# Cross attention with its exact fp32 products replaced by products of rounded high and low parts

## The chip, the core and the metric
One core of a Trainium2 chip runs the whole program. The metric is the device time of one execution in microseconds; the kernel before takes 1740.92 us (median of 3 runs, 1740.75 to 1741.70). The engines are TensorE (PE, matrix products, with its weight loads PEld), ScalarE (ACT), VectorE (DVE), GpSimd (POOL) and SyncE (SP, which issues the DMAs). They run side by side, each through its own list of instructions in order, and wait for each other with semaphores.

## The reference, cut to what matters
Two transformer blocks on 512 tokens of width 1024, all in fp32. The first has a gated feed-forward, a token mixer, cross attention to a memory of 256 rows, and a second feed-forward, each followed by a layer norm; the second has self attention with pooling and a feed-forward. The change is in the cross attention:

```
def _memory_cross_attention(h, mem, mem_g, mem_b, wq, wk, wv, wo):
    m = _layer_norm(mem, mem_g, mem_b)
    q = (h @ wq).reshape(B, T, 4, 256)
    k = (m @ wk).reshape(B, M, 4, 256)
    v = (m @ wv).reshape(B, M, 4, 256)
    s = jnp.einsum('bthd,bmhd->bhtm', q, k) * (256 ** -0.5)
    p = jax.nn.softmax(s, axis=-1)
    o = jnp.einsum('bhtm,bmhd->bthd', p, v).reshape(B, T, 1024)
    return o @ wo
```

## The kernel before
Activations lie turned: 128 features on the partitions, 512 tokens along the row, eight such tiles to a width of 1024. Every dense layer is a row of *blocks*. A block is one 128-column slice of a weight matrix; its output is one PSUM bank. Operands are kept in two rounded parts (type fp32r), high and low: `ahi` and `alo` for activations, `whi` and `wlo` for weights. A block's product is three rounded products for each of its 8 contraction tiles, 24 in all: `ahi` x `whi`, `alo` x `whi` (L434, L435) and `ahi` x `wlo` (L438); the first two blocks of a layer go together (L461, L462, L467).

Weights stream in by DMA into six slots `wraw`. ACT rounds a block to `whi` (L394, `hi_stream`), three blocks ahead of its use; then POOL (even blocks of these layers) or DVE (odd blocks) subtracts to get `wlo` (L399, `lo_stream`). Block outputs go round through banks 0 to 3; whoever empties a bank counts `bank_free`, and PE waits for it before it reuses the bank.

The stages around the change, in order, are the keys (`mk`, 8 blocks of 256 columns, the memory's rows), the values (`mv`, the same), the queries (`xq`, 8 blocks of 512 columns), the attention head, and the output projection (`xo`). The order of work on each engine is written out by hand.

- *Keys.* After each block DVE copies the bank to `kx` (L1828), makes its `wlo` (odd blocks), and does a piece of the second norm (`second_norm`). That norm is shared: DVE forms the variance (L1409, L1410), ACT takes logarithm and exponential (L1009, L1010); then for each of the 8 feature tiles DVE subtracts the mean (L1413) and multiplies (L1415), ACT applies gain and bias twice (L1015 to `ahi`, L1016 to `res`, "the pair"), and DVE forms `alo` (L1404). The tiles come in rounds 3, 5, 7, 9, 11, 12, 13 and 15 of the sixteen key and value blocks, on ACT one round later.
- *Values.* DVE copies the bank to `vxt` (L1835), PE turns it into bank 4 or 5 (L2298, `turn_values`, one block later), DVE copies the turned block to `vx` (L1839, L1842), counted by `s_kv`.
- *Queries.* DVE copies each block to `qx` with the scale 1/16 (L1874). After block 4 PE makes the scores of head 0, after block 7 it turns the probabilities of head 0.
- *The head.* For each of the four heads, numbered 0 to 3: *scores* (L2311, 8 exact fp32 products of 256 columns, `qx` by `kx`), maxima on DVE (L1847), exponentials on ACT (L1135), normalising on DVE (L1861, L1862), *turning* on PE (L2324, 8 transposes into banks 4 and 5), the turned halves copied to `pxT` (bank 4 by DVE, L1869; bank 5 by ACT, L1149), *attending* on PE (L2336, 4 exact products of 512 columns, `vx` by `pxT`), and its result rounded to `ahi` by ACT (L1143) and `alo` by DVE (L1854). In the trace each exact fp32 product shows as two passes, with two weight loads and two matmul records.

PE's order in the head is: turning 0, scores 1, scores 2, attend 0, turning 1, scores 3, turning 2, attend 1, turning 3, attend 2, attend 3, then xo. ACT's is: half 0, exponentials 1 and 2, attended 0, halves 1 and 2, exponentials 3, attended 1, half 3, attended 2 and 3. DVE's is: half 0, maxima 1, normalise 1, maxima 2, normalise 2, low part of attended 0, half 1, maxima 3, half 2, normalise 3, low part 1, half 3, low parts 2 and 3.

Of the kernel before, what the change touches and what calls it, by code (L numbers as in the profile page):

```python
# [92 lines left out]
def build(nc, A, out):  # L93
    ctx = ExitStack()
    with ctx:
# [110 lines left out]
        take = region(WORK)  # L206
        sst = take("sst", [P, QH, T], F32R)
# [418 lines left out]
        s_pca = sem("probabilities_copied_act")  # L626
        s_pv = sem("attended")
        s_ah = sem("attended_hi")

        s_rope = sem("rope_loaded")  # L630
        s_hsq = sem("head_squares")
# [215 lines left out]
        def _(act):  # L847
# [155 lines left out]
            def second_norm(m):  # L1003

                if m == 2:
                    act.wait_ge(stat_mean, 1)
                    act.activation(var[:, 0, :], mean_of("ln2"), ACT.Square).then_inc(mean_sq, 1)
                    act.wait_ge(var_ready, 1)
                    link(act.activation(rstd[:, :], var[:, 1, :], ACT.Ln, bias=small[:, S_EPS5:S_EPS5 + 1]))  # L1009
                    act.activation(square_mean_of("ln2"), rstd[:, :], ACT.Exp, scale=-0.5).then_inc(rstd_ready, 1)  # L1010
                if m - 1 in LN2_AT:
                    k = LN2_AT[m - 1]
                    act.wait_ge(scaled, k + 1)
                    g, b = vcol(V_LN2G + k), vcol(V_LN2B + k)
                    act.activation(ahi[:, k, :], res[:, k, :], ACT.Identity, bias=b, scale=g).then_inc(hi_act, 1)  # L1015
                    act.activation(res[:, k, :], res[:, k, :], ACT.Identity, bias=b, scale=g).then_inc(normed, 1)  # L1016
# [97 lines left out]
            for j in range(KD):  # L1114
                hi_stream(phases["out"], j)
                square_res(j, phases["out"])
                if j == MEM_AT:

                    act.wait_ge(s_mv, 1)
                    link(act.activation(mrs[:, :], mmv[:, :, 1], ACT.Ln, bias=small[:, S_EPS5:S_EPS5 + 1]))  # L1120
                    act.activation(mrs[:, :], mrs[:, :], ACT.Exp, scale=-0.5).then_inc(s_mr, 1)
                if j == MEM_AT + 1:

                    for k in range(KD):
                        act.wait_ge(s_ma, k + 1)
                        act.copy(mhi[:, k, :], mval[:, k % MVAL, :]).then_inc(s_mh, 1)
            for m in range(2 * KD):
                hi_stream(phases["mk"], m)
                second_norm(m)
            def cross_exp(h):  # L1130
                for t in range(TT):
                    act.wait_ge(s_nm, 2 * h + 2)
                    if t == 0 and h >= 2:
                        act.wait_ge(s_pT, 2 * (h - 1))
                    i = act.activation(px[:, h % 2, t, :], bank[SCORE_BANK[h] + t // 2][:, (t % 2) * MEM:(t % 2 + 1) * MEM],  # L1135
                                       ACT.Exp, bias=small[:, S_NM + 4 * (h % 2) + t:S_NM + 4 * (h % 2) + t + 1],
                                       accum_out=small[:, S_SM + 4 * (h % 2) + t:S_SM + 4 * (h % 2) + t + 1])
                    i.then_inc(s_pe, 1)
# [4 lines left out]
                    act.copy(ahi[:, 2 * h + d, :], bank[ATTEND_BANK[h] + d][:, :]).then_inc(s_ah, 1)  # L1143

            def take_turned(h):
                act.wait_ge(s_pT, 2 * h + 2)
                if h >= 2:
                    act.wait_ge(s_pv, 2 * (h - 1))
                act.copy(pxT[:, h % 2, 1, :], bank[5][:, :]).then_inc(s_pca, 1)  # L1149

            for j in range(KD):
                hi_stream(phases["xq"], j)
                second_norm(2 * KD + j)
                if j == 5:
                    cross_exp(0)
            take_turned(0)
            cross_exp(1)
            cross_exp(2)
# [199 lines left out]
        def _(dve):  # L1358
# [465 lines left out]
                                          vcol(V_MEMG + k), vcol(V_MEMB + k), ALU.mult, ALU.add).then_inc(s_ma, 1)  # L1824

            for j in range(KD):
                wait_block(dve, phases["mk"], j)
                dve.tensor_copy(kx[:, j, :], bank_of(phases["mk"], j)[:, 0:MEM]).then_inc(bank_free, 1)  # L1828
                lo_stream(phases["mk"], j)
                second_norm(j)  # L1830
            for j in range(KD):
                wait_block(dve, phases["mv"], j)
                if j >= 2:
                    dve.wait_ge(s_vxT, j - 1)
                dve.tensor_copy(vxt[:, j % 2, :], bank_of(phases["mv"], j)[:, 0:MEM]).then_inc(bank_free, 1)  # L1835
                lo_stream(phases["mv"], j)
                if j >= 1:
                    dve.wait_ge(s_vxT, j)
                    dve.tensor_copy(vx[:, :, (j - 1) * P:j * P], bank[4 + (j - 1) % 2][:, 0:MEM].rearrange("p (n f) -> p n f", f=P)).then_inc(s_kv, 1)  # L1839
                second_norm(KD + j)  # L1840
            dve.wait_ge(s_vxT, KD)
            dve.tensor_copy(vx[:, :, (KD - 1) * P:KD * P], bank[4 + (KD - 1) % 2][:, 0:MEM].rearrange("p (n f) -> p n f", f=P)).then_inc(s_kv, 1)  # L1842
            def cross_max(h):
                n0 = S_NM + 4 * (h % 2)
                dve.wait_ge(s_sc, h + 1)
# [17 lines left out]
                                      ALU.mult).then_inc(s_pn, 1)  # L1863

            def take_turned(h):
                dve.wait_ge(s_pT, 2 * h + 1)
                if h >= 2:
                    dve.wait_ge(s_pv, 2 * (h - 1))
                dve.tensor_copy(pxT[:, h % 2, 0, :], bank[4][:, :]).then_inc(s_pcd, 1)  # L1869

            for j in range(KD):
                wait_block(dve, phases["xq"], j)
# [130 lines left out]
        def _(pe):  # L2003
# [298 lines left out]
            def cross_scores(h):  # L2302
                if h == 0:
                    pe.wait_ge(bank_free, freed(phases["xq"], 1))
                elif h < 3:
                    pe.wait_ge(bank_free, freed(phases["xq"], last_block_in(phases["xq"], SCORE_BANK[h] + 1)))
                if h >= 2:
                    pe.wait_ge(s_pe, TT * (h - 1))
                for t in range(TT):
                    for k in range(2):  # L2310
                        i = pe.matmul(bank[SCORE_BANK[h] + t // 2][:, (t % 2) * MEM:(t % 2 + 1) * MEM],  # L2311
                                      qx[:, 2 * h + k, t * P:(t + 1) * P], kx[:, 2 * h + k, :], start=(k == 0), stop=(k == 1))
                i.then_inc(s_sc, 1)

            def cross_turn(h):
                pe.wait_ge(s_pn, TT * (h + 1))
                if h:
                    pe.wait_ge(s_pcd, h)
                    pe.wait_ge(s_pca, h)
                else:  # L2320
                    pe.wait_ge(s_kv, KD)
                for m in range(MT):
                    for t in range(TT):
                        i = pe.transpose(bank[4 + m][:, t * P:(t + 1) * P], px[:, h % 2, t, m * P:(m + 1) * P], ident)  # L2324
                    i.then_inc(s_pT, 1)

            def cross_attend(h):
                pe.wait_ge(s_pcd, h + 1)
                pe.wait_ge(s_pca, h + 1)
# [4 lines left out]
                for d in range(2):  # L2334
                    for m in range(MT):
                        i = pe.matmul(bank[ATTEND_BANK[h] + d][:, :], vx[:, m, (2 * h + d) * P:(2 * h + d + 1) * P], pxT[:, h % 2, m, :],  # L2336
                                      start=(m == 0), stop=(m == MT - 1))
                    i.then_inc(s_pv, 1)

            def first_head(j):  # L2340
# [63 lines left out]
            def self_turn(h, st):  # L2404
# [4 lines left out]
                        pe.wait_ge(bank_free, freed(phases["in2"], last_block_in(phases["in2"], 3)))  # L2409

                if st == 2:
                    pe.wait_ge(s_pcd, XH + h + 1)
                elif st == 3:
                    pe.wait_ge(s_pca, XH + 3 * h + 1)
                elif h:
                    pe.wait_ge(s_pca, XH + 3 * (h - 1) + 2 + st)
# [4 lines left out]
            def self_attend(h, st):  # L2421
# [1 line left out]
                if h < 0:  # L2423
                    return
                if st == 0:
                    pe.wait_ge(s_pcd, XH + h + 1)
                    pe.wait_ge(s_pca, XH + 3 * (h + 1))
# [47 lines left out]
```

## Time and profile before
| | |
|---|---|
| median of the runs | 1740.92 us (1740.75 to 1741.70) |
| the profiled execution | 1740.76 us |
| its span, first to last instruction | 1738.90 us, so 1.86 us lie around it |
| busy: PE, PEld, DVE, ACT, POOL | 98%, 82%, 39%, 34%, 41% of the span |
| mean granted clock of TensorE | 0.996 |

A busy share is a mean over stages with different limits. An engine's idle time in front of an instruction is put down to what released it. The chain of waits is followed back from the last instruction, at each step to what released it. In the timeline, rows of equal instructions are merged (x8), the first number is the start and the second the time until the end of the last. Since the matmuls overlap, their pace is read from one start to the next.

### The profile page before, as it was taken

The numbers are of one execution on the slowest core, as the hardware profiler recorded it, in microseconds if no ns is written. First come the engines' busy times: TensorE is split into PE (matmuls) and PEld (weight loads), VectorE is DVE, ScalarE is ACT, GpSimd is POOL, SyncE is SP. The second block draws the span as 40 slices with busy tenths as digits, with TensorE's granted clock in tenths as the row PEclk, the third lists the DMA queues.
The fourth block names the chain that finished last, engine by engine and source line by source line (L and its number), as shares of the span: only waits on it lengthen the run. The fifth ranks groups of instructions, "written<-read, shape, count | busy, mean of one in ns | idle before, by whom it ended". The sixth has DMA issues, their size and how long they took to land.

```text
span 1738.9 us, 21093 instructions
## 1 busy us (share of the span) xinstructions
PE 1701.5 (98%) x8525; PEld 1417.6 (82%) x8525; DVE 681.1 (39%) x1122; ACT 589.5 (34%) x890; POOL 710.9 (41%) x386
## 2 busy tenths in 40 slices
PE   7999999998999999999999999999899999999998
PEld 6888888897888789879888888898657988888886
DVE  3111211268776776356211121266884522112122
ACT  4222222256444554236222222246453422222210
POOL 3443444445554343114453444433331454444442
PEclk9999999999999999999999999999999999999999
DMA  6333243333222345212433233342111333323322
GB/s 189 97 97 97 79 116 97 97 110 85 61 61 61 97 125 142 73 49 71 112 97 97 82 112 97 86 128 61 37 37 49 85 98 97 97 82 112 97 85 73
DMA packets 302826, 157.66 MB, mean 91 GB/s; under 512 B 5145, under 2 KB 301194, under 8 KB 302730
## 3 DMA queue, kind: packets, MB, share of 16 engines
q1 hardware_dynamic: 302730, 156.32, 31.6%
q8 instruction: 68, 1.11, 0.3%
q14 instruction: 28, 0.23, 0.1%
HBM read 154.20 MB, written 2.10 MB: 90 GB/s over the span
## 4 chain that ended last, share of the span: by engine, by line
PE 66%; DVE 4%; ACT 3%; issue 2%; POOL 0%; DVEq 0%; ACTq 0%; POOLq 0%
PE bank L434 16%; PE bank L435 16%; PE bank L438 15%; PE bank L2430 1%; PE bank L2054 1%; PE bank L2051 1%; PE bank L2050 1%; PE bank L481 1%; PE bank L482 1%; PE bank L486 1%; PE bank L2206 1%; PE bank L467 1%; PE bank L461 1%; PE bank L462 1%; PE bank L2311 1%
## 5 line engine op out<-in xcount | busy, mean ns | idle before, releaser
L399 POOL TENSOR_TENSOR wlo<-wraw,whi 128x1024 fp32r<-128x1024 f32 (+1 forms) x256 | 608.6, 2390 | 909.9 <-ACT whi L394 909.9
L434 PE MATMUL bank<-ahi,whi 128*128 128x512 f32 x1312 | 516.0, 393 | 0.0
L435 PE MATMUL bank<-alo,whi 128*128 128x512 f32 x1312 | 511.7, 390 | 0.0
L394 ACT CAST whi<-wraw 128x1024 fp32r<-128x1024 f32 (+1 forms) x286 | 285.9, 1025 | 255.4 <-PE bank L438 169.4
L438 PE MATMUL bank<-ahi,wlo 128*128 128x512 f32 x1312 | 324.0, 389 | 0.0
L434 PEld LDWEIGHTS bank<-ahi,whi 128*128 128x128 f32 x1312 | 247.2, 188 | 52.1 <-issue 1.2
L435 PEld LDWEIGHTS bank<-alo,whi 128*128 128x128 f32 x1312 | 247.0, 188 | 52.0 <-issue 1.2
L438 PEld LDWEIGHTS bank<-ahi,wlo 128*128 128x128 f32 x1312 | 246.3, 188 | 51.1
L1377 DVE SCALAR_TENSOR_TENSOR hval<-gate,bank 128x512 f32<-128x512 f32 x66 | 45.4, 688 | 557.2 <-PE bank L438 543.2
L859 ACT ACTIVATE gate<-bank 128x512 f32<-128x512 f32 x66 | 39.6, 600 | 514.9 <-PE bank L438 506.1
L1386 DVE SCALAR_TENSOR_TENSOR res<-res,bank 128x512 f32<-128x512 f32 x80 | 54.1, 686 | 261.7 <-PE bank L438 181.7
L434 PE MATMUL bank<-hid,whi 128*128 128x512 f32 x332 | 130.5, 393 | 0.0
L435 PE MATMUL bank<-hid,whi 128*128 128x512 f32 x332 | 129.9, 391 | 0.0
L438 PE MATMUL bank<-hid,wlo 128*128 128x512 f32 x332 | 83.4, 391 | 0.0
L438 PEld LDWEIGHTS bank<-hid,wlo 128*128 128x128 f32 x332 | 62.3, 188 | 13.7
L434 PEld LDWEIGHTS bank<-hid,whi 128*128 128x128 f32 x332 | 62.4, 188 | 13.4
L435 PEld LDWEIGHTS bank<-hid,whi 128*128 128x128 f32 x332 | 62.4, 188 | 13.4
L1368 DVE TENSOR_TENSOR hid<-hval,hid 128x512 fp32r<-128x512 f32 x66 | 67.2, 1019 | 2.3
L876 ACT ACTIVATE gate<-res 128x256 f32<-128x256 f32 (+1 forms) x48 | 23.4, 488 | 120.5 <-DVE res L1386 66.7
L2050 PE MATMUL bank<-ahi,whi 128*128 128x256 f32 x256 | 63.3, 285 | 0.0
L2051 PE MATMUL bank<-alo,whi 128*128 128x256 f32 x256 | 62.8, 283 | 0.0
L481 PE MATMUL bank<-hid,whi 128*128 128x512 f32 x132 | 52.0, 394 | 0.0
(304 smaller groups left out, 2241.7 us busy)
## 6 DMA issues: line engine op xcount, KB each, us to landing
wraw<-in_ffn_w_gate SPq DMA_DIRECT2D x44, 512.0 KB, 3.8
wraw<-in_ffn_w_up SPq DMA_DIRECT2D x44, 512.0 KB, 3.8
wraw<-in_w_in SPq DMA_DIRECT2D x34, 512.0 KB, 3.9
wraw<-in_ffn_w_down SPq DMA_DIRECT2D x32, 512.0 KB, 4.0
wraw<-in_w_gate SPq DMA_DIRECT2D x22, 512.0 KB, 3.8
wraw<-in_w_up SPq DMA_DIRECT2D x22, 512.0 KB, 3.8
wraw<-in_w_out SPq DMA_DIRECT2D x16, 512.0 KB, 4.4
wraw<-in_w_down SPq DMA_DIRECT2D x16, 512.0 KB, 4.0
```

Of the source, the lines that this page charges most:

```text
L394: eng.copy(whi[:, b % 4, 0:n], wraw[:, b % RAW, 0:n]).then_inc(hi_ready, 1)
L399: eng.tensor_tensor(wlo[:, b % RAW, 0:n], wraw[:, b % RAW, 0:n], whi[:, b % 4, 0:n], ALU.subtract).then_inc(LO[b][0], 1)
L434: eng.matmul(o, w, xhi[:, k, :], start=(k == 0), stop=False)
L435: eng.matmul(o, w, xlo[:, k, :], start=False, stop=False)
L438: mm = eng.matmul(o, wlo[:, b % RAW, k * P:(k + 1) * P], xhi[:, k, :], start=False, stop=(k == ph.K - 1))
L481: eng.matmul(o, whi[:, b % 4, k * P:(k + 1) * P], hhi[:, k, :], start=(k == 0), stop=False)
L859: act.activation(gate[:, tile % 2, :], bank_of(ph, j)[:, :], ACT.Silu).then_inc(gate_done, 1)
L1368: dve.tensor_tensor(hlo[:, at, :], hval[:, tile % 2, :], hhi[:, at, :], ALU.subtract).then_inc(hidden_ready, 1)
L1377: dve.scalar_tensor_tensor(out=hval[:, tile % 2, :], in0=gate[:, tile % 2, :], scalar=scale, in1=bank_of(ph, j)[:, :], op0=ALU.mult, op1=A ...
L1386: dve.scalar_tensor_tensor(out=res[:, j, :], in0=res[:, j, :], scalar=scale, in1=bank_of(ph, j)[:, :], op0=ALU.mult, op1=ALU.add).then_inc ...
L2050: pe.matmul(o, w, xhi[:, k, at], start=(k == 0), stop=False)
L2051: pe.matmul(o, w, xlo[:, k, at], start=False, stop=False)
```

## The change
The exact products of the cross attention become three rounded ones each (high x high, high x low, low x high), so queries, keys, probabilities and values are all kept as a high and a low tile. ACT writes each high tile with a rounding copy from PSUM, DVE then subtracts it from the bank to get the low tile, and the bank is free only after DVE. The scale 1/16 goes from the queries to the keys. Values are split after their turning, two rounds after their block. Of the turned probabilities, ACT now rounds both halves and DVE subtracts both. In the second norm ACT waits for the variance one round later. The rest counts further where the numbers on a semaphore have doubled. The diff, cut to its core:

```
-        kx = take("kx", [P, KD, MEM])
-        vx = take("vx", [P, MT, D])
         vxt = take("vxt", [P, 2, MEM])
-        take = region(WORK + 48 * KB)
-        qx = take("qx", [P, KD, T])
+        kxhi, vxhi, qxhi, qxlo, kxlo, vxlo = ...   (fp32r, one after the other)
         px = take("px", [P, 2, TT, MEM])
-        pxT = take("pxT", [P, 2, MT, T])
+        pxhi = take("pxhi", [P, 2, MT, T], F32R)
+        pxlo = take("pxlo", [P, 2, MT, T], F32R)
...
ACT, second_norm:
                 if m == 2:
                     act.wait_ge(stat_mean, 1)
                     act.activation(var[:, 0, :], mean_of("ln2"), ACT.Square).then_inc(mean_sq, 1)
+                if m == 3:
                     act.wait_ge(var_ready, 1)
...
ACT, keys, values and queries:
+            def key_hi(j):
+                wait_block(act, phases["mk"], j)
+                act.activation(kxhi[:, j, :], bank_of(phases["mk"], j)[:, 0:MEM], ACT.Identity, scale=(D // XH) ** -0.5).then_inc(s_kxh, 1)
+            def query_hi(j):
+                wait_block(act, phases["xq"], j)
+                act.copy(qxhi[:, j, :], bank_of(phases["xq"], j)[:, :]).then_inc(s_qxh, 1)
+            def value_hi(j):
+                act.wait_ge(s_vxT, j + 1)
+                act.copy(vxhi[:, :, j * P:(j + 1) * P], bank[4 + j % 2]...).then_inc(s_vxh, 1)
             for m in range(2 * KD):
+                if 1 <= m <= KD:
+                    key_hi(m - 1)
                 hi_stream(phases["mk"], m)
+                if m >= KD + 2:
+                    value_hi(m - KD - 2)
                 second_norm(m)
+            for j in range(KD - 2, KD):
+                value_hi(j)
...
             def take_turned(h):
-                act.wait_ge(s_pT, 2 * h + 2)
                 if h >= 2:
                     act.wait_ge(s_pv, 2 * (h - 1))
-                act.copy(pxT[:, h % 2, 1, :], bank[5][:, :]).then_inc(s_pca, 1)
+                for m in range(MT):
+                    act.wait_ge(s_pT, 2 * h + m + 1)
+                    act.copy(pxhi[:, h % 2, m, :], bank[4 + m][:, :]).then_inc(s_pca, 1)
             for j in range(KD):
                 hi_stream(phases["xq"], j)
                 second_norm(2 * KD + j)
+                if j:
+                    query_hi(j - 1)
                 if j == 5:
                     cross_exp(0)
+            query_hi(KD - 1)
...
DVE, keys, values, turned probabilities, queries:
-                wait_block(dve, phases["mk"], j)
-                dve.tensor_copy(kx[:, j, :], ...).then_inc(bank_free, 1)
+                dve.wait_ge(s_kxh, j + 1)
+                dve.scalar_tensor_tensor(out=kxlo[:, j, :], in0=bank_of(phases["mk"], j)[:, 0:MEM], scalar=(D // XH) ** -0.5,
+                                         in1=kxhi[:, j, :], op0=ALU.mult, op1=ALU.subtract).then_inc(bank_free, 1)
...
-                if j >= 1:
-                    dve.wait_ge(s_vxT, j)
-                    dve.tensor_copy(vx[:, :, (j - 1) * P:j * P], ...).then_inc(s_kv, 1)
+                if j >= 2:
+                    value_lo(j - 2)
...
-                dve.tensor_copy(pxT[:, h % 2, 0, :], bank[4][:, :]).then_inc(s_pcd, 1)
+                for m in range(MT):
+                    dve.wait_ge(s_pca, 2 * h + m + 1)
+                    dve.tensor_tensor(pxlo[:, h % 2, m, :], bank[4 + m][:, :], pxhi[:, h % 2, m, :], ALU.subtract).then_inc(s_pcd, 1)
...
-                dve.tensor_scalar(qx[:, j, :], bank_of(phases["xq"], j)[:, :], (D // XH) ** -0.5, None, ALU.mult).then_inc(bank_free, 1)
+                dve.wait_ge(s_qxh, j + 1)
+                dve.tensor_tensor(qxlo[:, j, :], bank_of(phases["xq"], j)[:, :], qxhi[:, j, :], ALU.subtract).then_inc(bank_free, 1)
...
PE, scores and attending:
-                    for k in range(2):
-                        i = pe.matmul(..., qx[:, 2 * h + k, t * P:(t + 1) * P], kx[:, 2 * h + k, :], ...)
+                    for k in range(2 * h, 2 * h + 2):
+                        pe.matmul(o, qxhi[:, k, at], kxhi[:, k, :], start=(k == 2 * h), stop=False)
+                        pe.matmul(o, qxhi[:, k, at], kxlo[:, k, :], start=False, stop=False)
+                        i = pe.matmul(o, qxlo[:, k, at], kxhi[:, k, :], start=False, stop=(k == 2 * h + 1))
...
                     for m in range(MT):
-                        i = pe.matmul(..., vx[:, m, ...], pxT[:, h % 2, m, :], ...)
+                        pe.matmul(o, vxhi[:, m, at], pxhi[:, h % 2, m, :], start=(m == 0), stop=False)
+                        pe.matmul(o, vxhi[:, m, at], pxlo[:, h % 2, m, :], start=False, stop=False)
+                        i = pe.matmul(o, vxlo[:, m, at], pxhi[:, h % 2, m, :], start=False, stop=(m == MT - 1))
```

## Rows read from the trace of the kernel before

**Rows 1.** The page's first part: busy us, share of the span, instructions
```profile
PE 1701.5 (98%) x8525; PEld 1417.6 (82%) x8525; DVE 681.1 (39%) x1122; ACT 589.5 (34%) x890; POOL 710.9 (41%) x386
```

**Rows 2.** By stretch: us, busy PE PEld DVE ACT POOL, clock, DMA share, GB/s
```profile
656.00:681.00 25.00, 24.30 (x194) 23.28 (x194) 20.54 (x34) 15.58 (x19) 9.85 (x4) 1.00 0.61 171
...
725.40:753.40 28.00, 27.54 (x113) 18.20 (x111) 15.02 (x33) 11.73 (x35) 0.00 (x0) 1.00 0.07 20
```

**Rows 3.** Chain of waits in order of time: start us, us, what
```profile
637.85 0.94 PE bank L438 x8
...
698.58 1.81 PE bank L438 x8
...
726.52 6.91 PE bank L2311 x32
733.42 3.43 PE bank L2336 x8
...
742.68 1.95 ACT px L1135 x8
744.86 1.15 DVE px L1862 x4
```

**Rows 4.** Timeline of DVE, key stage: start, us, instruction, [idle before <-releaser]
```profile
639.17 1.22 DVE L399 TENSOR_TENSOR wlo<-wraw,whi 128x1024 fp32r<-128x1024 f32 x1
640.30 0.69 DVE L1409 TENSOR_TENSOR hval<-bank,hval 128x512 f32<-128x512 f32 x1
...
647.31 0.42 DVE L1828 COPY kx<-bank 128x256 f32<-128x256 f32 x1
647.65 0.68 DVE L1413 TENSOR_TENSOR res<-res,bank 128x512 f32<-128x512 f32 x1
648.36 0.69 DVE L1415 TENSOR_TENSOR res<-res,bank 128x512 f32<-128x512 f32 x1
...
650.48 1.22 DVE L399 TENSOR_TENSOR wlo<-wraw,whi 128x1024 fp32r<-128x1024 f32 x1
```

**Rows 5.** Timeline of ACT, key stage
```profile
642.24 0.60 ACT L1010 ACTIVATE bank<-rstd 128x512 f32<-128x512 f32 x1
...
644.67 0.81 ACT L1015 ACTIVATE ahi<-res,vecs 128x512 fp32r<-128x512 f32 x1
645.38 0.80 ACT L1016 ACTIVATE res<-res,vecs 128x512 f32<-128x512 f32 x1
```

**Rows 6.** Timeline of DVE, the head
```profile
739.12 1.28 DVE L1854 TENSOR_TENSOR alo<-bank,ahi 128x512 fp32r<-128x512 f32 x2
740.32 0.68 DVE L1869 COPY pxT<-bank 128x512 f32<-128x512 f32 x1
```

**Rows 7.** Timeline of PE at five places
```profile
489.29 2.00 PE L2206 MATMUL bank<-qt,kt 128*128 128x64 f32 x16 [1.01 <-DVE kt L1667]
...
652.76 0.28 PE L461 MATMUL bank<-mhi,whi 128*128 128x256 f32 x1
...
678.02 0.44 PE L2298 MATMUL bank<-mats,vxt 128*128 128x128 f32 x2 [0.30 <-DVE vxt L1835]
...
741.10 1.06 PE L2324 MATMUL bank<-mats,px 128*128 128x128 f32 x8
...
746.06 1.09 PE L2324 MATMUL bank<-mats,px 128*128 128x128 f32 x8 [0.46 <-DVE px L1862]
...
753.46 0.79 PE L461 MATMUL bank<-ahi,whi 128*128 128x512 f32 x1
```

**Rows 8.** One line's instructions on ACT: duration ns min/median/max, first and last start
```profile
L1126 ACT CAST mhi<-mval x8: 406/407/408, 622.1 to 626.1; 128x256 fp32r<-128x256 f32 x8
...
L1149 ACT COPY pxT<-bank x4: 586/586/628, 726.6 to 747.2; 128x512 f32<-128x512 f32 x4
```

**Rows 9.** Busy time and clock by stretch, after the wait at 488 us
```profile
492.00:494.00 2.00, 2.00 (x12) 2.00 (x11) 1.50 (x4) 0.00 (x0) 0.00 (x0) 0.50 0.03 8
494.00:496.00 2.00, 2.00 (x11) 1.87 (x11) 0.05 (x1) 0.58 (x1) 0.55 (x2) 0.66 0.00 0
```

More of the change, by code:

```diff
@@ L196, in build @@
         mval = take("mval", [P, MVAL, MEM])
-        kx = take("kx", [P, KD, MEM])
-        vx = take("vx", [P, MT, D])
         vxt = take("vxt", [P, 2, MEM])
-        take = region(WORK + 48 * KB)
-        qx = take("qx", [P, KD, T])
+        kxhi = take("kxhi", [P, KD, MEM], F32R)
+        vxhi = take("vxhi", [P, MT, D], F32R)
+        qxhi = take("qxhi", [P, KD, T], F32R)
+        qxlo = take("qxlo", [P, KD, T], F32R)
+        kxlo = take("kxlo", [P, KD, MEM], F32R)
+        vxlo = take("vxlo", [P, MT, D], F32R)
         take = region(WORK)
         px = take("px", [P, 2, TT, MEM])
-        pxT = take("pxT", [P, 2, MT, T])
+        pxhi = take("pxhi", [P, 2, MT, T], F32R)
+        pxlo = take("pxlo", [P, 2, MT, T], F32R)
         take = region(WORK)
@@ L628, in build @@
         s_ah = sem("attended_hi")
+        s_vxh = sem("memory_values_hi")
+        s_kxh = sem("memory_keys_hi")
+        s_qxh = sem("memory_queries_hi")
         s_rope = sem("rope_loaded")
@@ L1126, in _ @@
                         act.copy(mhi[:, k, :], mval[:, k % MVAL, :]).then_inc(s_mh, 1)
+            def key_hi(j):
[6 more added lines that the diff above has]
+                act.wait_ge(s_vxT, j + 1)
+                act.copy(vxhi[:, :, j * P:(j + 1) * P], bank[4 + j % 2][:, 0:MEM].rearrange("p (n f) -> p n f", f=P)).then_inc(s_vxh, 1)
             for m in range(2 * KD):
+                if 1 <= m <= KD:
+                    key_hi(m - 1)
                 hi_stream(phases["mk"], m)
+                if m >= KD + 2:
+                    value_hi(m - KD - 2)
                 second_norm(m)
+            for j in range(KD - 2, KD):
+                value_hi(j)
             def cross_exp(h):
@@ L1826, in _, with value_lo @@
             for j in range(KD):
-                wait_block(dve, phases["mk"], j)
-                dve.tensor_copy(kx[:, j, :], bank_of(phases["mk"], j)[:, 0:MEM]).then_inc(bank_free, 1)
+                dve.wait_ge(s_kxh, j + 1)
+                dve.scalar_tensor_tensor(out=kxlo[:, j, :], in0=bank_of(phases["mk"], j)[:, 0:MEM], scalar=(D // XH) ** -0.5,
+                                         in1=kxhi[:, j, :], op0=ALU.mult, op1=ALU.subtract).then_inc(bank_free, 1)
                 lo_stream(phases["mk"], j)
                 second_norm(j)
+            def value_lo(j):
+                at = slice(j * P, (j + 1) * P)
+                dve.wait_ge(s_vxh, j + 1)
+                dve.tensor_tensor(vxlo[:, :, at], bank[4 + j % 2][:, 0:MEM].rearrange("p (n f) -> p n f", f=P), vxhi[:, :, at],
+                                  ALU.subtract).then_inc(s_kv, 1)
             for j in range(KD):
@@ L1836, in _ @@
                 lo_stream(phases["mv"], j)
-                if j >= 1:
-                    dve.wait_ge(s_vxT, j)
-                    dve.tensor_copy(vx[:, :, (j - 1) * P:j * P], bank[4 + (j - 1) % 2][:, 0:MEM].rearrange("p (n f) -> p n f", f=P)).then_inc(s_kv, 1)
+                if j >= 2:
+                    value_lo(j - 2)
                 second_norm(KD + j)
-            dve.wait_ge(s_vxT, KD)
-            dve.tensor_copy(vx[:, :, (KD - 1) * P:KD * P], bank[4 + (KD - 1) % 2][:, 0:MEM].rearrange("p (n f) -> p n f", f=P)).then_inc(s_kv, 1)
+            for j in range(KD - 2, KD):
+                value_lo(j)
             def cross_max(h):
@@ L2309, in cross_scores @@
                 for t in range(TT):
-                    for k in range(2):
-                        i = pe.matmul(bank[SCORE_BANK[h] + t // 2][:, (t % 2) * MEM:(t % 2 + 1) * MEM],
-                                      qx[:, 2 * h + k, t * P:(t + 1) * P], kx[:, 2 * h + k, :], start=(k == 0), stop=(k == 1))
+                    o, at = bank[SCORE_BANK[h] + t // 2][:, (t % 2) * MEM:(t % 2 + 1) * MEM], slice(t * P, (t + 1) * P)
+                    for k in range(2 * h, 2 * h + 2):
+                        pe.matmul(o, qxhi[:, k, at], kxhi[:, k, :], start=(k == 2 * h), stop=False)
+                        pe.matmul(o, qxhi[:, k, at], kxlo[:, k, :], start=False, stop=False)
+                        i = pe.matmul(o, qxlo[:, k, at], kxhi[:, k, :], start=False, stop=(k == 2 * h + 1))
                 i.then_inc(s_sc, 1)
@@ L2334, in cross_attend @@
                 for d in range(2):
+                    o, at = bank[ATTEND_BANK[h] + d][:, :], slice((2 * h + d) * P, (2 * h + d + 1) * P)
                     for m in range(MT):
-                        i = pe.matmul(bank[ATTEND_BANK[h] + d][:, :], vx[:, m, (2 * h + d) * P:(2 * h + d + 1) * P], pxT[:, h % 2, m, :],
-                                      start=(m == 0), stop=(m == MT - 1))
+                        pe.matmul(o, vxhi[:, m, at], pxhi[:, h % 2, m, :], start=(m == 0), stop=False)
+                        pe.matmul(o, vxhi[:, m, at], pxlo[:, h % 2, m, :], start=False, stop=False)
+                        i = pe.matmul(o, vxlo[:, m, at], pxhi[:, h % 2, m, :], start=False, stop=(m == MT - 1))
                     i.then_inc(s_pv, 1)
@@ L2411, in self_turn @@
                 if st == 2:
-                    pe.wait_ge(s_pcd, XH + h + 1)
+                    pe.wait_ge(s_pcd, 2 * XH + h + 1)
                 elif st == 3:
-                    pe.wait_ge(s_pca, XH + 3 * h + 1)
+                    pe.wait_ge(s_pca, 2 * XH + 3 * h + 1)
                 elif h:
-                    pe.wait_ge(s_pca, XH + 3 * (h - 1) + 2 + st)
+                    pe.wait_ge(s_pca, 2 * XH + 3 * (h - 1) + 2 + st)
                 for t in range(TT):
@@ L2425, in self_attend @@
                 if st == 0:
-                    pe.wait_ge(s_pcd, XH + h + 1)
-                    pe.wait_ge(s_pca, XH + 3 * (h + 1))
+                    pe.wait_ge(s_pcd, 2 * XH + h + 1)
+                    pe.wait_ge(s_pca, 2 * XH + 3 * (h + 1))
                     if h >= 4 and h % 2 == 0:
```

8 lines of the change are left out of this document (2 added, 6 removed).

## The prediction

> **What bounds the kernel now.** The page's first part comes first: TensorE (PE) is busy for 1701.5 of 1738.9 us [rows 1]. That alone would say that every PE nanosecond saved is won. So the second view is the busy time by stage. In the value stage PE is busy for 24.3 of 25.0 us, in the attention head for 27.54 of 28.0, at a granted clock of 1.00 (2.4 GHz) [rows 2]. Third is the chain of waits in order of time [rows 3]. It gives the pace of each kind of product (time of a piece over its count), and it shows where PE does not set the time: in the head, before the turning of head 3, the chain leaves PE for ACT (1.95 us of exponentials) and DVE (1.15 us of normalising). There PE looks full because its own work happens to be as long as the relay ACT to DVE to PE beside it. Last come the timelines of DVE and ACT in the key stage [rows 4, 5] and of DVE in the head [rows 6], for the steps of those relays.
>
> The profiled run took 1740.76 us: the span of 1738.90 and 1.86 around it. The median of the runs is 1740.92, 0.16 more. My sum is a difference at one point, the start of the output projection xo (753.46 us in the trace [rows 7]); after it both kernels run the same instructions with the same waits. I add the difference to the median.
>
> **PE work removed.** An exact fp32 product runs as two passes. A score pass (256 columns) takes 6.91/32 = 0.216 us, an attend pass (512 columns) 3.43/8 = 0.429 [rows 3]. A rounded product of 256 columns takes 0.94/8 = 0.118, of 512 columns 1.81/8 = 0.226 [rows 3]. Scores of a head: 16 passes x 0.216 = 3.45 become 24 x 0.118 = 2.83, so -0.62. Attend of a head: 8 x 0.429 = 3.43 become 12 x 0.226 = 2.72, so -0.71. Four heads: -5.3 us of PE work. What follows is how much of it reaches xo.
>
> **Key stage: a new relay, +1.35.** Now DVE alone empties a key bank, 0.34 us from start to start [rows 4]. After the change ACT rounds the bank first and DVE subtracts. No row has ACT's form (256 columns from PSUM, scaled, rounded out); the nearest are the rounding copy of 256 columns from SBUF, 0.41, and the 512-column copy from PSUM, 0.59 [rows 8]. I take 0.42, since the width is that of the first. By the Trainium skill's page "ScalarE: Activation LUTs", section "What ACT_TABLE_LOAD costs", an ACTIVATE with immediate scale takes 186 ns and 0.833 ns per column, an estimate of 0.40 here; no row here shows it, and the term below would be 0.08 smaller. DVE's subtraction has one operand in PSUM and one in SBUF. At 512 columns that form takes 0.69 [rows 4], hardly more than the plain copy's 0.68 [rows 6]; so I price it like the copy that it replaces, next start after 0.34.
> Behind these waits on DVE are queued its own halves of weight blocks and the second norm, on ACT the rounding of weights and the gain-and-bias pairs of the norm (0.71 us from start to start [rows 5]), each pair waiting for DVE. The two engines now wait for each other in turn:
> - Key 2 reaches DVE 0.45 later (ACT's 0.42 and the hop), and with it the weight half that starts at 639.17 and the variance behind it. Ln and Exp on ACT end at 642.84 now [rows 5], at 643.3 then. (That ACT waits for the variance one block later only keeps the order free of a circle.)
> - Only then ACT rounds key 3, until 643.65. DVE: key 3, subtract, multiply (0.34 + 0.71 + 0.69 [rows 4]) until 645.4.
> - ACT: pair until 646.9, key 4 until 647.3. DVE: key 4, weight half (1.13 to the next start [rows 4]), key 5, subtract, multiply (0.34 + 1.13 + 0.34 + 0.71 + 0.69) until 650.5.
> - ACT: pair until 652.0, key 6 until 652.4. DVE: key 6, weight half of value block 1 (0.34 + 1.22) until 654.0; PE sees it at 654.1.
> PE starts the values at 652.76 [rows 7]. Now that half is done at 650.48 + 1.22 = 651.7 [rows 4]: a cover of 1.06 us, which is used up, and PE waits 1.35. Bounds: nothing, if the relay fits; and at the 512-column prices of ACT's 0.81 from SBUF and DVE's 0.69 [rows 4, 5], four key steps x 0.40 and five x 0.26 more, a wait of 4.25. I stay near the 256-column row.
>
> **Value stage: +0.32.** PE turns value block i after the products of block i+1, once block i-2 has left the same bank. Till now DVE copied block i-2 out in its round for block i-1; now ACT rounds it and DVE subtracts it in the round for block i. For all but the last turning a block's 24 x 0.118 = 2.83 us of products cover that. The last one, of block 7, follows at once on the one before: it waits 0.30 for DVE's copy of block 7 now [rows 7], and then besides for DVE's subtraction of block 5, which stands behind that copy, 0.32. Bounds 0 and 0.6.
>
> **Query stage: -0.62.** PE's scores of head 0 shrink. ACT's rounding (0.59, a 512-column copy from PSUM [rows 8]) now precedes DVE's 0.69 in each block of 24 x 0.226 = 5.4 us, and three other banks are free: hidden; uncovered it would be 0.6 a block. The weight roundings that ACT issues behind it are needed three blocks later. PE is then 1.35 + 0.32 - 0.62 = 1.05 late at turning 0.
>
> **The head: the relay, not PE.** Scores 1 end another 0.62 sooner, so the relay starts 0.43 late. It is maxima, exponentials (1.95), normalising (1.15), the same for head 2, low parts of the attended values (1.28), then the turned probabilities of head 1 [rows 3, 6]. Till now DVE copied one half (0.68) while ACT copied the other; then ACT rounds both and DVE subtracts both: one more 0.61 on DVE, while ACT's halves lie under DVE's low parts. Turning 2, at 741.10 now [rows 7], begins 0.43 + 0.61 = 1.04 late. PE gets there 2.7 us early and waits. Turning 2 to turning 3 is a relay again (ACT's halves, exponentials, normalising): ACT begins on the first half 0.44 sooner, but has a second one of 0.50, +0.06. So turning 3 is 1.1 late. After it PE sets the pace with two attends, -1.42.
> Edits with no cost: the counters of self attention only count further, and the new tiles lie in space for which no new wait is made.
>
> **Sum.** 1.35 + 0.32 - 0.62 - 0.62 + 0.61 + 0.06 - 1.42 = -0.3 us. Half of the 5.3 us of PE work (attends 0 and 1, scores 2 and 3) is done faster only to wait; the other half, 2.7, is met by 2.3 of new waits. 1740.92 - 0.3 = **1740.6**.
>
> **The rivals.**
> - *All PE savings count*: -5.3, 1735.6. For it: PE is nearly always busy, and its longest wait in the head is 0.46 us [rows 7]. Against it: the chain's pieces on ACT and DVE [rows 3]. 7%.
> - *No wait in the key stage*, the rest as above: -0.3 - 1.35 = -1.65, 1739.3. It holds if ACT gets its keys in while DVE works. 8%.
> - *The clock falls* after PE's wait before turning 2. After a wait of 1.01 us in this trace [rows 7] the granted clock read 0.50 and 0.66 in two slices of 2 us [rows 9]: 2 x 0.50 + 2 x 0.34 = 1.7 us lost; after 0.46 us in the head it stayed at 1.00 [rows 2]. Falling over attends 2 and 3 it costs 1.7, over attend 1 nearly nothing, for a wait follows. -0.3 + 1.7 = +1.4, 1742.3. The Trainium skill, "TensorE: Matmul & The Clock Gate", section "HAM oscillation — how this bites in real kernels", says that idle gaps between bursts of matmuls put the engine back to the slow clock; by that rule it is this case. 19%.
> - *The relay costs more than the products give* (slower): the key steps at the 512-column prices, PE waiting 4.25 us before the values, -0.3 + 2.9 = +2.6, and after so long a wait the clock's 1.7: +4.3, 1745.2. It decides from about 0.8 us for ACT's and 0.7 for DVE's step of 256 columns. Against it: the 0.41 row. 9%.
> - *The rounded products don't run at the rounded pace*: scores at 24 x 0.216 = 5.18 a head, +1.7 instead of -0.6, some +6 in all, 1747. Against it: the key stage's products have this very form [rows 3]. 1%.
> - The forecast: 56%.
>
> **How the numbers follow.** A difference under 0.2% (3.5 us) can't be told from none here. Faster by that: only the first rival, 7%. Slower: the last two, 10%. Within it: the rest, 83%. The range takes in the missing key wait (1739.3) less 0.5 for the products' pace, and on the other side the fallen clock (1742.3) with 1.1 for the key steps' bounds: 1738.8 to 1743.4.
>
> **What would show it.** The key relay: PE waiting about 1.3 us for DVE's weight half at the first value block, and ACT's key roundings at 0.42. The head: PE waiting some 2.7 us before turning 2 and 1.4 before turning 3, both for DVE. Products 0.118 and 0.226 apart; the granted clock at 1.00 from 740 to 760 us; xo starting at 753.2. What would make me wrong above all is a step of 256 columns far from 0.42, which is met nine times in the key relay, and the clock.

## The result, and the profile after

The changed kernel takes 1743.26 us (median of 22 runs, 1741.70 to 1744.48) against 1740.88 (1740.16 to 1742.30, 22 runs): 1.0013 times as long, 95% interval 1.0007 to 1.0018. It is 2.4 us slower where the forecast was 0.3 faster. The profiled execution took 1743.52 us, its span is 1741.7.

The page's first part, which answers to [rows 1]: PE is busy for 3.5 us less, with its time at the lower clock (below) counted in, and for a smaller share of a longer span.

```profile
PE 1698.0 (97%) x8573; PEld 1421.5 (82%) x8573; DVE 692.1 (40%) x1126; ACT 599.4 (34%) x918; POOL 710.2 (41%) x386
```

PE's waits from 620 to 760 us (total, times, longest). Before, that stretch had two for `vxt` (0.7 together) and the one before turning 3 [rows 7]:

```profile
PE bank L464 <- DVE wlo L402: 2.6, 1, 2.6
PE bank L2360 <- DVE pxlo L1905: 2.4, 1, 2.4
PE bank L2360 <- DVE px L1897: 1.2, 1, 1.2
PE bank L2333 <- DVE vxlo L1864: 0.6, 1, 0.6
PE bank L2333 <- DVE vxt L1871: 0.4, 1, 0.4
```

The same places in PE's timeline, beside [rows 7]:

```profile
655.30 0.54 PE L464 MATMUL bank<-mhi,whi 128*128 128x256 f32 x1 [2.63 <-DVE wlo L402]
...
745.14 1.06 PE L2360 MATMUL bank<-mats,px 128*128 128x128 f32 x8 [2.41 <-DVE pxlo L1905]
...
750.22 1.09 PE L2360 MATMUL bank<-mats,px 128*128 128x128 f32 x8 [1.24 <-DVE px L1897]
```

Executions differ by up to 2 us in when they reach the key stage (624.8 to 626.8), from work that no kernel here changes. Behind the stretch they differ too: from the start of xo to the end it is 984.9 to 986.6 us. So I compare the stretch from the first key product to the first product of xo, stage by stage. Turning 0, turning 2 and xo are taken where the chain of waits has them (754.02 for xo in the kernel before), since the record of a product that follows another at once can begin while that one still runs (753.46 in [rows 7]). The first row is the profile before, the second the result's profile, the third another profile of the changed kernel (E1 below). Us:

| | keys | values | queries | turning 0 to 2 | 2 to 3 | 3 to xo | sum |
|---|---|---|---|---|---|---|---|
| before | 26.05 | 25.61 | 47.27 | 15.55 | 4.87 | 7.96 | 127.31 |
| after | 28.83 | 27.64 | 46.69 | 15.51 | 5.08 | 6.55 | 130.30 |
| after, E1 | 28.82 | 26.11 | 46.68 | 15.51 | 5.08 | 6.57 | 128.77 |
| forecast of the difference | +1.35 | +0.32 | -0.62 | -0.01 | +0.06 | -1.42 | -0.3 |
| E1 less before | +2.77 | +0.50 | -0.59 | -0.04 | +0.21 | -1.39 | +1.46 |

Two numbers are off: the keys by 1.4 us, in both profiles, and the values by 1.7, in one of them. Of the second, 1.5 is the clock. The busy time and granted clock by stretch (us, PE, PEld, DVE, ACT, POOL, clock, DMA share, GB/s), the result's profile:

```profile
654.00:656.00 2.00, 0.70 (x3) 0.73 (x4) 1.98 (x3) 1.61 (x3) 1.53 (x1) 0.83 0.85 249
656.00:658.00 2.00, 2.00 (x12) 2.00 (x11) 1.82 (x2) 1.26 (x2) 1.29 (x1) 0.50 0.02 5
658.00:660.00 2.00, 2.00 (x16) 2.00 (x16) 0.00 (x0) 0.25 (x1) 0.00 (x0) 0.82 0.00 0
```

and E1's, over the same products:

```profile
655.00:660.00 5.00, 5.00 (x45) 5.00 (x43) 1.90 (x3) 1.52 (x2) 1.38 (x1) 1.00 0.01 2
```

Behind the wait before the values TensorE ran at its lower level (0.50, so 1.2 GHz) in the first and stayed at 2.4 GHz in the second. The products start 0.21 us apart there (655.64, 655.85, 656.07) instead of 0.12.

Why the wait is 2.6 and not 1.35 stands in the timelines of the key stage. The variance's last step on DVE, in the kernel before, where it follows the second row of [rows 4]:

```profile
641.02 0.43 DVE L1410 TENSOR_SCALAR hval<-hval 128x512 f32<-128x512 f32 x1
```

The same engine in the changed kernel:

```profile
640.47 0.68 DVE L1438 TENSOR_TENSOR hval<-bank,hval 128x512 f32<-128x512 f32 x1
641.19 1.91 DVE L1439 TENSOR_SCALAR hval<-hval 128x512 f32<-128x512 f32 x1
644.83 0.42 DVE L1857 SCALAR_TENSOR_TENSOR kxlo<-bank,kxhi 128x256 fp32r<-128x256 f32 x1 [1.73 <-ACT kxhi L1136]
```

ACT in the changed kernel, beside [rows 5]:

```profile
638.86 1.04 ACT L397 CAST whi<-wraw 128x1024 fp32r<-128x1024 f32 x1
643.14 0.72 ACT L1016 ACTIVATE rstd<-hval,small 128x512 f32<-128x512 f32 x1 [3.23 <-DVE hval L1439]
643.89 0.60 ACT L1017 ACTIVATE bank<-rstd 128x512 f32<-128x512 f32 x1
644.43 0.37 ACT L1136 ACTIVATE kxhi<-bank 128x256 fp32r<-128x256 f32 x1
```

POOL, the changed kernel too:

```profile
639.98 2.84 POOL L402 TENSOR_TENSOR wlo<-wraw,whi 128x1024 fp32r<-128x1024 f32 x1 [3.58 <-ACT whi L397]
```

The step L1439 reads and writes one 512-column tile in SBUF. It has the operands it always had, and takes 1.91 us instead of 0.43. It ends at 643.10, 0.28 after POOL's subtraction (639.98 + 2.84 = 642.82). In the kernel before, that subtraction started later:

```profile
643.88 2.42 POOL L399 TENSOR_TENSOR wlo<-wraw,whi 128x1024 fp32r<-128x1024 f32 x1 [7.66 <-ACT whi L394]
```

### The profile page after: what moved, and what is told of

Same layout as the page of the kernel before. It is cut to its first block, busy times and chain, and to the rows that moved or that the text cites. A ratio compares the mean times of both kernels' runs of the same rounds, so it can differ in the third digit from the quotient of the medians.

```text
span 1741.7 us, 21220 instructions
## 1 busy us (share of the span) xinstructions
PE 1698.0 (97%) x8573; PEld 1421.5 (82%) x8573; DVE 692.1 (40%) x1126; ACT 599.4 (34%) x918; POOL 710.2 (41%) x386
## 4 chain that ended last, share of the span: by engine, by line
PE 65%; DVE 5%; ACT 4%; issue 2%; POOL 0%; DVEq 0%; ACTq 0%; POOLq 0%
PE bank L437 15%; PE bank L438 15%; PE bank L441 15%; PE bank L2467 1%; PE bank L2089 1%; PE bank L2086 1%; PE bank L2085 1%; PE bank L484 1%; PE bank L485 1%; PE bank L489 1%; PE bank L2241 1%; PE bank L464 1%; PE bank L470 1%; PE bank L465 1%; ACT res L905 1%
## 5 line engine op out<-in xcount | busy, mean ns | idle before, releaser
L1397 DVE TENSOR_TENSOR hid<-hval,hid 128x512 fp32r<-128x512 f32 x66 | 71.5, 1083 | 2.3
```

What stands on the lines that cost most here:

```text
L1397: dve.tensor_tensor(hlo[:, at, :], hval[:, tile % 2, :], hhi[:, at, :], ALU.subtract).then_inc(hidden_ready, 1)
```

## The theories

*The collision (mine).* The line that moves Ln and Exp one round later also lets ACT's rounding of a weight block (638.86) go ahead of ACT's wait for the variance. So POOL starts on that block before DVE's last variance step, and DVE is held until POOL is through. ACT's Ln, Exp and next key wait for DVE, DVE's next key for ACT: the 1.48 us go down the key relay to PE. *The rival:* the relay of key roundings is longer than forecast in itself, and the long step is covered by other waits. *Beside both:* the clock falls behind the long wait in some executions; and, for the head, the relay sets the time and not PE (mine) or PE does.

Each kernel was run beside the kernel before; a ratio is against that. E1, E2, E4 and E5 shared a chip, then E3 and E6 to E8, then E9 to E12.

## The experiments

**E1, E9, E10. The changed kernel again**, no edit.

> The kernel after once more, as the reference of this group. Its trace showed TensorE waiting 2.63 us for DVE's weight half before the values (1.35 were forecast), and then products of 256 columns 0.214 us apart for 3.5 us (granted clock 0.50). Theory A (key relay, port and clock): the same here, +1.5 to +3.2 us against the kernel before, the spread coming from how much of the slow clock falls on products. Theory B (the head: two low halves for DVE instead of one copy): the same total, and nothing in the key stage changes it.

1742.42 us, ratio 1.0011 (1.0003 to 1.0020). PE waits 2.62 before the values, the clock stays up, and the stretch is 128.77.

> The kernel after a third time. In the two profiles so far the wait before the values was 2.63 and 2.62 us; the clock fell behind it in one (256-column products 0.214 us apart) and not in the other, and the stretch from the first key product to xo took 130.3 and 128.8 us. Theory A: the wait is 2.6 again and the stretch takes one of these two values, by the clock alone. If it takes a third, something else varies.

> The same kernel, one more profile: wait 2.6 us, the stretch 128.8 or 130.3 us, with the clock.

E9: 1743.68, ratio 1.0017 (1.0007 to 1.0026). E10, one run: 1741.71. Both profiles have the wait of 2.62 and the clock fallen behind it, stretches of 130.27 and 130.18. Of four profiles of this kernel three show the fall, at the same place, and all four the same waits.

**E2, E11. No collision.** The changed kernel, but POOL holds back its half of key block 6 until the variance is there:

```
             for name in ("mk", "mv", "xq"):
                 for j in range(KD):
+                    if name == "mk" and j == 3:
+                        pool.wait_ge(var_ready, 1)
                     lo_stream(phases[name], j)
```

> Only POOL waits for the variance before it makes the low half of the weights of key block 6, so that this step no longer runs beside DVE's last variance step. Theory A, with the rival on the shared SBUF access as its part: that DVE step takes 0.43 us instead of 1.91, the wait before the values falls from 2.63 to about 1.2, a gain of 1.4; if the clock no longer falls after so short a wait, another 1.5: 0 to +1.6 us against the kernel before. If POOL's step has nothing to do with the 1.91 us, the step and the wait stay. Theory B: no change against the kernel after.

> The kernel without the collision, a second profile: DVE's last variance step 0.43 us, the wait before the values 1.1 us, the stretch 127.3 us.

E2: 1740.63, ratio 1.0000 (0.9991 to 1.0009); E11, one run: 1741.08. Timeline of DVE in E2:

```profile
639.81 0.43 DVE L1441 TENSOR_SCALAR hval<-hval 128x512 f32<-128x512 f32 x1
```

POOL there:

```profile
640.31 2.42 POOL L402 TENSOR_TENSOR wlo<-wraw,whi 128x1024 fp32r<-128x1024 f32 x1 [5.29 <-DVE hval L1441]
```

And PE, at the first value product:

```profile
652.43 0.36 PE L464 MATMUL bank<-mhi,whi 128*128 128x256 f32 x1 [1.14 <-DVE wlo L402]
```

The step is back at 0.43, the wait falls by 1.49 to 1.14, the key stage is 27.35 (27.34 in E11), the stretch 127.30 (127.18). So the collision is worth 1.48 us, and what is left of the key relay is +1.30 against the kernel before, where 1.35 was forecast. The clock stays up in both. The ratios' intervals of E1 and E2 overlap (1.0003 to 1.0020 and 0.9991 to 1.0009); the stage times carry the verdict, and the medians, 1.8 us apart, go the same way.

**E3. The collision alone**, in the kernel before: Ln and Exp one round later, nothing else.

```
                     act.activation(var[:, 0, :], mean_of("ln2"), ACT.Square).then_inc(mean_sq, 1)
+                if m == 3:
                     act.wait_ge(var_ready, 1)
```

> The kernel before with one edit of the change alone: ACT takes Ln and Exp of the variance one round later, behind the rounding of key weight block 6. No relay on the keys. Theory A: POOL's weight half now starts beside DVE's last variance step, which takes 1.9 us instead of 0.43, but DVE empties its banks alone and has 1.06 us of cover before the values, so TensorE waits 0 to 0.5 us: within 0.5 us of the kernel before. Rival: the longer variance step is itself what costs, +1.5 us.

1742.19, ratio 1.0001 (0.9992 to 1.0009). The collision comes, by the same amount. DVE in E3:

```profile
639.34 1.92 DVE L1411 TENSOR_SCALAR hval<-hval 128x512 f32<-128x512 f32 x1
```

POOL in E3:

```profile
638.34 2.63 POOL L399 TENSOR_TENSOR wlo<-wraw,whi 128x1024 fp32r<-128x1024 f32 x1 [3.79 <-ACT whi L394]
```

DVE ends at 641.26, 0.29 after POOL (640.97). PE's waits are those of the kernel before and the stretch is 127.30 against 127.31. The one line is harmless where DVE empties the banks alone: the cover of 1.06 us before the values and a later hold that goes away take it up (DVE's half at 644.82 in the kernel before took 2.56 us beside POOL's of 643.88; in E3 it starts at 643.70 and takes 1.22). Only with the relay of keys behind it does the line cost anything. Neither part alone gives the loss in the stretch. The medians are no evidence here: E3's is 1.04 above that of the kernel before in its group (1741.15), because six of E3's eleven runs lie at 1742.19 to 1742.57, and nine of 33 of the kernel before lie up there as well; the profile is of a run from the lower group.

**E4. Keys rounded by DVE, and Ln and Exp back in their round.** On the changed kernel:

```
ACT:
-                if m == 3:
-                if 1 <= m <= KD:
-                    key_hi(m - 1)
DVE, keys:
+                wait_block(dve, phases["mk"], j)
+                dve.tensor_scalar(kxhi[:, j, :], bank_of(phases["mk"], j)[:, 0:MEM], (D // XH) ** -0.5, None, ALU.mult).then_inc(s_kxh, 1)
```

> The key stage's relay undone: DVE alone makes the high and the low part of each key block (two steps of 0.42 us), ACT does nothing there and waits for the variance where the kernel before does. The rest as after. Theory A: no wait before the values and no fall of the clock, so the rest of the change shows alone: 1.6 us faster than the kernel before (-0.3 forecast less the 1.35 of the wait), about 4 faster than after. Theory B: no change against the kernel after, +2.4 against before.

1739.56, ratio 0.9993 (0.9984 to 1.0002). No wait before the values, key stage 26.12: relay and collision are both gone, at 0.44 to 0.46 us more of DVE a key, from start to start. The stretch is 126.88; it would be 0.8 less (turning 2 to 3 took 5.84 us, not 5.08), but in this profile the clock fell at turning 2. PE's timeline, where the eight transposes take 1.94 us instead of 1.06:

```profile
740.34 1.94 PE L2355 MATMUL bank<-mats,px 128*128 128x128 f32 x8 [2.40 <-DVE pxlo L1900]
```

**E5. The wait before the values filled**, to take only the clock's part away. On the changed kernel, 21 products that nobody reads (added work):

```
+            pe.wait_ge(s_ma, KD)
+            for n in range(21):
+                pe.matmul(bank[5][:, 0:MEM], mhi[:, 0, 0:P], mhi[:, 1, :], start=True, stop=True)
             linear("mv", lambda k: (s_ml, KD), mhi, mlo, MEM, after=turn_values)
```

> The wait before the values is kept, but 21 extra rounded products of 256 columns (2.5 us) into an unused bank keep TensorE busy in it. They compute nothing that is used. Theory A: TensorE has work until DVE's half is there, the clock stays at 1.00, and the 1.5 us that it cost come back: about +1 us against the kernel before, 1.5 faster than after. If the slow clock costs nothing on the path, this kernel is as slow as after or slower.

1742.32, ratio 1.0009 (1.0001 to 1.0018); its neighbour E1 had 1742.42. The values run at full clock (25.89), but the clock falls at turning 2 (granted 0.70 from 745 to 750), and the stretch is 128.68. The gain expected in the median did not come. Each run's mean granted clock is on record, and by it E1's profile is not typical of E1: it is the fastest of eleven runs, alone at 0.997, and the other ten have 0.995 (1742.32 to 1743.84). E5's runs have 0.993 to 0.995, but for one of 0.997, its fastest (1740.98). A mean does not say where the clock fell. So E5 shows the filling in its own stage, where the clock stayed up, but not what the clock at the values is worth in the median: turning 2 and stages outside the stretch can have taken it back.

**E6. The head's order.** E2's kernel, with the turned probabilities of head 1 ahead of the attended values of head 0:

```
ACT:  cross_exp(2)
-     attended_hi(0)
      take_turned(1)
+     attended_hi(0)
DVE:  cross_normalise(2)
-     attended_lo(0)
      take_turned(1)
      cross_max(3)
+     attended_lo(0)
```

> The kernel without the collision (e2), and in the head DVE and ACT take the turned probabilities of head 1 before the attended values of head 0. If the relay of ACT and DVE sets the head's time, turning 2 comes 1.2 us sooner (DVE's two low parts of 0.6 move out of its way) and so does everything after it: 1739.4 us. Rival, TensorE's own work sets it: no change against e2.

1740.31, ratio 0.9992 (0.9983 to 1.0001). Turning 0 to 2 takes 14.32 instead of 15.51, and PE's wait before turning 2 halves, as its timeline shows:

```profile
739.70 1.06 PE L2362 MATMUL bank<-mats,px 128*128 128x128 f32 x8 [1.22 <-DVE pxlo L1907]
```

The stretch is 126.03, 1.27 less than E2's. The profile is of one of the five faster runs (1738.30 to 1739.39; the other six have 1740.31 to 1740.97), but E8 and E12 have the same turning 0 to 2, 14.32 and 14.31. The relay ACT to DVE sets turning 2: with PE's work the same, 1.2 us less in front of `pxlo` is 1.2 us less at PE.

**E7. Attend 0 done twice.** E2's kernel, PE doing 2.73 us more in the head (the semaphore counts only the second time; that part of the edit is left out here):

```
-                for d in range(2):
+                for d in (0, 1, 0, 1) if h == 0 else (0, 1):
```

> The kernel without the collision (e2), but TensorE makes the 12 products of attend 0 twice (2.73 us more of its work; the second time is the one that is used). Its wait before turning 2 is 2.41 us. If that part of the saving only became waiting, it costs 0.3 us: 1740.9. Rival, every TensorE nanosecond counts: +2.7, 1743.4.

1742.02, ratio 1.0001 (0.9992 to 1.0010). The stretch grows by 0.12 to 127.42, and the wait before turning 2 is gone from PE's waits (620 to 760 us):

```profile
PE bank L2362 <- DVE px L1899: 1.3, 1, 1.3
PE bank L464 <- DVE wlo L402: 1.2, 1, 1.2
PE bank L2335 <- DVE vxlo L1866: 0.6, 1, 0.6
PE bank L2335 <- DVE vxt L1873: 0.4, 1, 0.4
```

So 2.6 of 2.73 us of PE work are free there, and the rounded attend 0 saved nothing. This is one profile; the median of E7 is 0.87 above that of the kernel before in its group.

**E8, E12. Three reliefs at once:** E4, E6's order, and DVE subtracting value block 5 before it copies block 7.

```
             for j in range(KD):
+                if j == KD - 1:
+                    value_lo(j - 2)
                 wait_block(dve, phases["mv"], j)
...
-                if j >= 2:
+                if 2 <= j < KD - 1:
                     value_lo(j - 2)
```

> The kernel after with three reliefs: DVE alone splits the keys (e4), the order in the head of e6, and DVE subtracts value block 5 before it copies block 7. From e4 (1.1 us faster than the kernel before) less 1.2 for the head and 0.5 for the value wait: 1737.9 us, 2.8 faster than before. Theory A asks for this. Rival: what is taken from one relay comes back in the next wait, and it stays near e4, 1739.6.

> The kernel with the three reliefs once more: the stretch 125.0 us, the whole 2.3 to 3.1 us faster than the kernel before.

E8: 1738.02, ratio 0.9983 (0.9974 to 0.9992). E12: 1737.78, ratio 0.9986 (0.9976 to 0.9996). Stretches 124.98 and 124.91, so 2.4 less than before. PE's waits in E8, the same stretch:

```profile
PE bank L2357 <- DVE px L1894: 1.2, 1, 1.2
PE bank L2357 <- DVE pxlo L1902: 1.2, 1, 1.2
PE bank L2330 <- DVE vxt L1868: 1.1, 2, 0.7
```

The third relief brought nothing: the value stage is 26.17 against 26.12 in E4. DVE's steps only changed places, and the last turning now waits 0.65 for the copy of block 7 instead of 0.55 for the subtraction of block 5. The other two hold in both runs: this is the version that beats the kernel before, by 0.14 to 0.17%.

## Why the forecast was wrong

**The step that failed** is in the key stage: "Key 2 reaches DVE 0.45 later (ACT's 0.42 and the hop), and with it the weight half that starts at 639.17 and the variance behind it. Ln and Exp on ACT end at 642.84 now [rows 5], at 643.3 then. (That ACT waits for the variance one block later only keeps the order free of a circle.)" I took the variance's steps at their old durations, and did not ask what ACT does in the round it gains. It rounds a weight block, this starts POOL 3.7 us earlier than before (639.98 against 643.88, in a profile whose key stage starts 0.24 earlier), and POOL holds DVE: Exp ended at 644.49. Set at the start of the key stage in the kernel before, this is 644.73, 1.4 past the forecast. In E2, with POOL held back, it ended at 641.62, which is 643.25 on the same footing: the forecast's 643.3. The rest of the relay was right: +1.30 in E2 for +1.35. It was right step by step and not by errors that cancel: on that footing the two multiplies end at 645.33 and 650.40 (645.4 and 650.5 forecast), and PE starts the values at 654.06 (654.1). The rival "relay costs more" had the sign, but the wrong mechanism: it wanted 0.8 us for ACT's and 0.7 for DVE's step. The steps of one line, over the stage (duration min, median, max in ns, first and last start), ACT's:

```profile
L1136 ACT ACTIVATE kxhi<-bank x8: 360/377/388, 632.2 to 654.3; 128x256 fp32r<-128x256 f32 x8
```

and DVE's:

```profile
L1857 DVE SCALAR_TENSOR_TENSOR kxlo<-bank,kxhi x8: 418/424/426, 632.6 to 655.0; 128x256 fp32r<-128x256 f32 x8
```

0.42 was assumed for ACT (0.04 too much), and DVE's copy of the same width took 0.42 before. The Trainium skill, "ScalarE: Activation LUTs", section "What ACT_TABLE_LOAD costs", by which I had estimated 0.40, was nearer.

**The clock.** "The clock falls" was a rival with 19%, placed at turning 2 at a price of 1.7 us. It fell behind the wait before the values, in three of four profiles of the changed kernel, and cost 1.5 us there (27.64 less 26.11). Here is a second gap in the prediction: it had PE wait 1.35 us before the values and priced no fall of the clock there, though [rows 9] show one behind a wait of 1.01 us. That the failed step made the fall likelier, by a wait of 2.6 instead of 1.35, is not shown: behind 1.1 to 1.2 us at the same place (E2, E6, E7, E11) it fell in none of four, but four profiles against four are few, and the last section has a short wait behind which it mostly falls. At turning 2, behind 2.4 us, it fell in two of eight profiles (E4, E5). There it cost 0.8 and 0.3 us before turning 3, since a wait follows, as the prediction's "over attend 1 nearly nothing" had it in part.

**The values**, +0.32 forecast, are +0.50. The last turning waits 0.55 for `vxlo`, where 0.30 + 0.32 = 0.62 were added up, so this place gives 0.25. Another 0.13 lies before the turning of block 6 and 0.08 at the stage's first products (E4 has both too, without a wait before the stage); what causes these two is not traced.

**The queries**: -0.62 forecast, -0.59 measured. The rounded scores run at the rounded pace, ACT's rounding of each query block is hidden.

**The head** was right in its mechanism and nearly so in size. Waits of 2.41 and 1.24 us before turnings 2 and 3 (2.7 and 1.4 forecast), turning 2 to 3 +0.21 (for +0.06), the two attends that count -1.39 (for -1.42). E7 shows that attend 0's saving is worth nothing, E6 that the relay decides. The rival "all PE savings count" (-5.3) is out.

**The sum.** With the collision taken out it is -0.01 us in E2's stretch and a ratio of 1.0000, for -0.3 forecast. The collision adds 1.48, which gives E1's +1.46. The fallen clock adds 1.5 more, +3.0 in the result's profile. The medians (+2.4, +1.8 in E1, +3.2 in E9) lie between or near these two, which agrees with a fall in some executions and not in others. The mean granted clocks point the same way: in the result's 22 runs it is 0.997 in three, which are the three fastest (1741.70 to 1741.83), and 0.995 in the other nineteen (1742.09 to 1744.48, median 1743.52). By that the slower course is the usual one. But this is an inference. The mean takes in other places where the clock falls (E1's profile lacks one near 492 us too, which the result's profile has), and in the runs of the kernel before beside E1 it goes from 0.993 to 0.996 without the times following.

## What to carry over

When a wait is moved later on an engine, price what that engine does in the time it gains, and follow each result to whoever starts on it: here one line on ACT moved a POOL instruction by 3.7 us onto a DVE step on the critical path. A step's duration is only as good as its neighbours: before you reuse a row's time, list what DVE and POOL do beside it before and after. Where PE looks full in a relay, work saved on PE is turned into waiting, and the same microsecond is to be had by reordering the engines that it waits for.

## What the hardware showed

An SBUF-to-SBUF step on DVE stops while POOL runs a subtraction over SBUF operands: 0.43 us became 1.91 in all four profiles of the changed kernel and 1.92 in E3, each ending 0.28 or 0.29 after POOL. One input in SBUF is enough for that: the step has a single operand and a constant. It is not any DVE step: the one in front of it (L1438, one operand in PSUM, one in SBUF) runs wholly beside the same POOL step and takes 0.68 us, against 0.69 in [rows 4]. The `alo` subtractions of the norm, with two SBUF inputs, meet it too. One line's instructions on DVE in the changed kernel (duration ns min, median, max), of which the first takes 1.25 us beside a POOL step that ends at 652.25:

```profile
L1433 DVE TENSOR_TENSOR alo<-res,ahi x8: 685/1062/1431, 651.6 to 685.8; 128x512 fp32r<-128x512 f32 x8
```

It goes both ways: POOL's step takes 2.84 us in the changed kernel, starting at 639.98 while DVE's weight half runs until 640.56, and 2.42 in E2, where it starts behind DVE's step. The Trainium skill states the rule, "SBUF — State Buffer", section "SBUF: two separate sides": VectorE, in a two-port mode or with two SBUF inputs (the latter only against a GpSimd step that reads SBUF), and GpSimd share a pair of ports as "an exclusive lock, not a bandwidth split", and who starts first has it for the whole instruction. The traces agree: who starts second is held, to within 0.2 us until the other is through. In which mode L1439 ran no trace shows.

The clock did not follow the length of the wait alone. One and the same kernel had it fall behind 2.6 us in E9 and E10 and not in E1. Before turning 2, behind 2.4 us, it fell in two of eight profiles. And near 488 us, in a stage that no kernel here changes, PE waits 0.98 to 1.01 us in all 14 profiles (the first row of [rows 7]); there it fell in twelve, all but those of E1 and E3. From 492 to 494 us the granted clock is 0.50 in [rows 9] and 1.00 in E1.
